# Expert weights in 1 MB chunks: a ring of 18 single slots in place of nine double ones

## The chip, the core and the metric

The kernel runs on one core of one Trainium2 chip. The metric is device time in microseconds of one execution, from three runs: median 1295.08 us, 1293.2 to 1295.19. Profiles are taken in a separate execution. Everything is in float32. In this text 1 MB is 1,048,576 bytes (the profile's own "MB" are 1,000,000 bytes).

## The reference

One layer over 256 latent tokens and 256 context tokens of width 1024. A mixer (a bidirectional gated linear recurrence beside a pooling branch) comes first; then a mixture of 32 experts, of which each token takes four. Every expert gets some tokens, so all of their weights are read: `w1` is 1024 x 2048, `w2` 1024 x 1024, 12 MB per expert, 384 MB in all.

```python
def moe(h, w_r, b_r, w1, b1, w2, b2):
    logits = (h @ w_r + b_r).astype(jnp.float32)
    top_v, top_i = lax.top_k(logits, TOP_K)
    top_w = jax.nn.softmax(top_v, axis=-1)
    comb = jnp.einsum('nk,nke->ne', top_w, jax.nn.one_hot(top_i, N_EXPERTS, dtype=jnp.float32)).astype(h.dtype)
    out = jnp.zeros_like(h)
    for e in range(N_EXPERTS):
        z = h @ w1[e] + b1[e]
        glu = jnp.minimum(z[:, :D_FF], SWIGLU_LIMIT)
        lin = jnp.clip(z[:, D_FF:], -SWIGLU_LIMIT, SWIGLU_LIMIT)
        act = glu * jax.nn.sigmoid(SWIGLU_ALPHA * glu) * (lin + 1)
        out = out + comb[:, e:e + 1] * (act @ w2[e] + b2[e])
    return out
```

## The kernel before

The kernel is written engine by engine, with semaphores between them; nothing reorders it. Its first 360 us are the mixer and the router. Then TensorE (`pe`) goes through 33 items. An item is one expert with up to 64 of its tokens; one expert with more tokens than that is run twice, as items 15 and 16, on weights loaded once.

In an item TensorE multiplies the gathered tokens `xg` with `w1` (`first_map`, 32 matmuls; the profile counts each float32 matmul twice, so 64), scatters the item before into the output sums (`scatter`), gathers the next item's tokens (`gather`), turns the activations of this one (`item`, L934) and multiplies them with `w2` (`second_map`, 16 matmuls). The last item does its second map in two halves of the output columns (`second_map_halves`). DVE and ACT compute SwiGLU in between.

Weights come through `arena`, 18 slots of 1 MB (8 KB in each of 128 partitions). `PAIRS` names nine pairs of neighbouring slots, which become a ring; an expert is six chunks of 2 MB (`CPI = 6`), four of `w1` and two of `w2`. In a `w1` chunk each partition holds two neighbouring rows of `w1`, in a `w2` chunk four of `w2`, so that a partition reads 16 KB in one piece (`expert_src`). That fixes which channels stand in which partition, and the transposes of tokens and activations pick their columns with a step of 2 or 4 to match.

SyncE (`sp`) issues all the expert loads in order, on one queue. Load n goes into pair n mod 9, and its semaphore `expert_landed[n mod 9]` is what TensorE waits for before the chunk's first matmul. TensorE counts `w_used` up after a chunk's last matmul, and SyncE waits for that count before it issues the load that takes the chunk's place. While the mixer runs, the slots hold other things, so the first nine loads wait for those one after another (L427 to L453): the last of them for the end of the output projection and for the tokens' normalisation. From the third expert on SyncE needs the routing result first (`items_ready`, L457). GpSimd loads 16 chunks of `w_mod` during the mixer on its own queue (L520), 8 KB in each partition; `w_in` comes in rows of 1 KB (L426), `w_out` in rows of 4 KB (L437).

Of the kernel before, what the change touches and what calls it, by code (L numbers as in the profile page):

```python
# [12 lines left out]
ds = bass.ds  # L13

P = 128
D = 1024
KT = D // P
# [12 lines left out]
SLOTS = 64  # L30
MORE = 16
FILL = (3, 1, 2)
CPI = 6
FETCHED = 2
TWICE = 15
NP = E + 1
# [7 lines left out]
CW = KT * CHUNK  # L44
BANK = 512
HALF = 512
NSLOT = 18
ACC, TMP, WIN, UT, XC, M2, ROWS_AT = 0, 2, 6, 8, 10, 16, 17
RING_SLOTS = [12, 13, 14, 15]
RING = len(RING_SLOTS)  # L50
MOD_SLOTS = [ACC, ACC + 1, TMP, TMP + 1, M2, ROWS_AT, TMP + 2, TMP + 3]
OUT_SLOTS = [XC, XC + 1, ACC, ACC + 1]
PAIRS = [UT, WIN, TMP, TMP + 2, RING_SLOTS[2], RING_SLOTS[0], XC, ACC, M2]
WSLOTS = len(PAIRS)
RING_CHUNKS = 4 + 2 * HEADS + 4 + 12 + 1 + 8
GM_SLOTS = [ROWS_AT, M2, XC, XC + 1]
GM_AT = [0, 1, 0, 1, 0, 1, 0, 2, 3, 0, 2, 3, 0, 2, 3, 0]
# [34 lines left out]
def build(nc, I, out):  # L92
    ctx = ExitStack()
    with ctx:
# [9 lines left out]
        def slot(n, w=CW):  # L104
            return arena[:, n * CW:n * CW + w]
# [61 lines left out]
        o = WIN * CW  # L167
# [14 lines left out]
        brow = {g: arena[:, TMP * CW + n * D:TMP * CW + (n + 1) * D] for n, g in enumerate(("g1", "sh2", "sc2", "g2"))}  # L182
        nrow = {g: arena[:, TMP * CW + (n + 4) * D:TMP * CW + (n + 5) * D] for n, g in enumerate(("g1", "sc2", "g2"))}

        wpair = [arena[:, n * CW:(n + 2) * CW] for n in PAIRS]
        w1_at = [w.rearrange("p (r n) -> p r n", r=2) for w in wpair]
        w2_at = [w.rearrange("p (r n) -> p r n", r=4) for w in wpair]

        sh2rw = RB[:, 0:KT * E].rearrange("p (k e) -> p k e", k=KT)
        sh2sum = RB[:, KT * E:KT * E + E]  # L190
# [140 lines left out]
        def chunk_used(n):  # L331

            kind, m = next(key for key, c in chunk_no.items() if c == n)
            if kind == "lru":
                return gates_done, m + 1
            if kind == "xr" and m == 0:
                return rows_used, 1
            if kind == "xr" and m == 1:
                return job_done, number["xr", 3] + 1
            if kind in ("xr", "pw"):  # L340
                m += {"xr": 1, "pw": 3}[kind]
            return job_done, number[kind, m] + 1
# [17 lines left out]
        def slot_of(i, c):  # L360

            return load_no(i, c) % WSLOTS

        def landed_at(i, c):

            if isinstance(i, int):
                return 16 * (load_no(i, c) // WSLOTS + 1)
            return i * 16 + 16 * ((LAST + c) // WSLOTS + 1 - FIXED)

        def expert_src(e, c):  # L370

            if c < 4:
                return I["exp_w1"][0, ds(e, 1), c * 256:(c + 1) * 256, :].rearrange("a (p r) n -> p (a r) n", r=2)
            return I["exp_w2"][0, ds(e, 1), (c - 4) * 512:(c - 3) * 512, :].rearrange("a (p r) n -> p (a r) n", r=4)

        def load_vectors(eng, names):

# [17 lines left out]
        def _(sp):  # L395
            def load_expert(q, e, c):
                s = (q * CPI + c) % WSLOTS
                sp.dma_start((w1_at if c < 4 else w2_at)[s], expert_src(e, c)).then_inc(expert_landed[s], 16)

            def load_mod(g):  # L400

# [11 lines left out]
            for n, parts in enumerate(chunks):  # L413
                if n < 2:
                    load_mod(n)
                if n >= RING:
                    sp.wait_ge(*chunk_used(n - RING))
                at = RING_SLOTS[n % RING] * CW
                for src, o in parts:
                    w = int(np.prod(src.shape)) // P  # L420
                    dst = arena[:, at + o:at + o + w]
                    if len(src.shape) == 4:
                        dst = dst.rearrange("p (g k n) -> p g k n", g=src.shape[1], k=src.shape[2])
                    else:
                        dst = dst.rearrange("p (k n) -> p k n", k=src.shape[1])
                    sp.dma_start(dst, src).then_inc(ring_landed[n % RING], 16)  # L426
                if n == chunk_no["pp", 2]:  # L427
                    sp.wait_ge(job_done, number["mp", 3] + 1)
                    load_expert(0, 0, 0)
                if n == chunk_no["pp", 3]:  # L430
                    sp.wait_ge(job_done, number["pw", 3] + 1)
                    load_expert(0, 0, 1)
                if n == chunk_no["rp", 0]:
                    sp.wait_ge(job_done, number["rs", 5] + 1)
                    sp.wait_ge(g2_part, 1)
                    for c in range(4):
                        sp.dma_start(wo_w[c], I["w_out"][0, c * 256:(c + 1) * 256, :].rearrange(  # L437
                            "(k p) n -> p k n", p=P)).then_inc(wo_landed, 16)
            sp.wait_ge(rows_ready, 1)
            load_expert(0, 0, 2)  # L440
            load_expert(0, 0, 3)
            sp.wait_ge(*chunk_used(chunk_no["rp", 1]))
            sp.wait_ge(*chunk_used(chunk_no["rp", 2]))
            load_expert(0, 0, 4)
            sp.wait_ge(*chunk_used(chunk_no["rp", 3]))
            load_expert(0, 0, 5)
            sp.dma_start(x1, I["x"][0].rearrange("(t p) d -> p t d", p=P)).then_inc(xres_landed, 16)
            sp.wait_ge(wo_done, 2 * TT)
            load_expert(1, 1, 0)
            load_expert(1, 1, 1)  # L450
            sp.wait_ge(ssq3_ready, 2 * TT)
            sp.wait_ge(v_ready, TT)
            load_expert(1, 1, 2)  # L453
            sp.dma_start(b2s, I["exp_b2"][0]).then_inc(b2_landed, 16)
            for q in range(1, E - 1):
                if q == FETCHED:
# [93 lines left out]
        def _(pe):  # L550
# [244 lines left out]
            def first_turn(q):  # L795

                pe.wait_ge(xgt_ready, q + 1)
                if q:
                    bank_read(7)
                for j in range(2 * q, 2 * q + 2):  # L800
                    last = nc.tensor.transpose(psum[1 + 6 * q][:, j * P:(j + 1) * P], xgt[:, q * 256 + j % 2:q * 256 + 256:2], ident[:, :])
                last.then_inc(xT_done, 1)

            def gather(n):
# [9 lines left out]
            def turn_tokens(n):  # L814

                pe.wait_ge(xgt_ready, n + 2)
                b = psum[4]
                for j in range(4):
                    last = nc.tensor.transpose(b[:, j * P:(j + 1) * P], xgt[:, j // 2 * 256 + j % 2:j // 2 * 256 + 256:2], ident[:, :])  # L819
                last.then_inc(xT_done, 1)  # L820

            def first_map(i, first=False):

                for c in range(4):
                    if first and c == 1:
                        turn_weights()
                        pe.wait_ge(xg_ready, 2)
                    s = slot_of(i, c)
                    pe.wait_ge(expert_landed[s], landed_at(i, c))
                    for r in range(2):  # L830
                        k = 2 * c + r
                        for q in range(2):
                            for h in range(2):
                                o = q * D + h * HALF
                                last = mm(psum[4 + q][h * SLOTS:(h + 1) * SLOTS, :], xg[:, k // 4, k % 4, :],  # L835
                                          w1_at[s][:, r, o:o + HALF], start=False, stop=(k == KT - 1))
                    last.then_inc(w_used, 1)

            def second_map(i):

                for c in range(2):
                    s = slot_of(i, 4 + c)
                    pe.wait_ge(expert_landed[s], landed_at(i, 4 + c))
                    for r in range(4):
                        for h in range(2):
                            last = mm(psum[6][h * SLOTS:(h + 1) * SLOTS, :], actT[:, c, r, :],  # L846
                                      w2_at[s][:, r, h * HALF:(h + 1) * HALF], start=(c == 0 and r == 0), stop=(c == 1 and r == 3))
                    last.then_inc(w_used, 1)

            def second_map_halves(i):  # L850

                for q in range(2):
                    for c in range(2):
                        s = slot_of(i, 4 + c)
                        if q == 0:
                            pe.wait_ge(expert_landed[s], landed_at(i, 4 + c))
                        for r in range(4):
                            for h in range(2):
                                o = h * HALF + q * 256
                                last = mm(psum[6 + q][h * SLOTS:(h + 1) * SLOTS, 0:256], actT[:, c, r, :], w2_at[s][:, r, o:o + 256],  # L860
                                          start=(c == 0 and r == 0), stop=(c == 1 and r == 3))
                    last.then_inc(y_half, 1)

            def scatter_halves(n):
# [48 lines left out]
            def item(i, first=False, last=False):  # L913
# [17 lines left out]
                if first:  # L931
                    pe.wait_ge(items_ready, 1)
                for j in range(4):
                    turned = nc.tensor.transpose(psum[7][:, j * P:(j + 1) * P], actf[:, j:HALF:4], ident[:, :])  # L934
                turned.then_inc(actT_done, 1)
                if not last:
                    turn_tokens(i + 1)
# [262 lines left out]
        def _(dve):  # L1200
# [366 lines left out]
            def item(i, last=False):  # L1567
# [5 lines left out]
                if not last:  # L1573
# [9 lines left out]
                    else:  # L1583
                        dve.wait_ge(gather_done, i)
                    one_hot(e1, r1)
                dve.wait_ge(w_used, i * CPI + 4)
                v.tensor_scalar(glu, psum[4][:, :], LIMIT, None, ALU.min).then_inc(glu_ready, 1)  # L1587
                step(v.tensor_scalar(lin, psum[5][:, :], LIMIT, -LIMIT, ALU.min, ALU.max), 1)
                dve.wait_ge(glu_ready, i + 1)
# [81 lines left out]
```

## Time and profile before

| | |
|---|---|
| median of 3 runs | 1295.08 us |
| the profiled execution's own time | 1293.98 us |
| its span, first to last instruction | 1291.7 us |
| granted TensorE clock, mean | 0.997 |
| TensorE busy | 1254.9 us, 97% of the span |
| DVE / ACT / GpSimd busy | 352.0 / 216.8 / 30.6 us |
| moved by DMA | 476.03 MB (of 1,000,000 bytes) |
| SyncE's queue alone | 454.23 MB, 85.4% of 16 engines' span |
| chain that ended last | PE 77%, DMA 14%, ACT 4%, DVE 4% |

The chain is followed back from the last instruction; its DMA part is the loads of expert weights (13%), its largest TensorE part the first map (L835, 28%) and the second map (L846, 15%). A busy TensorE is one that has matmuls in flight; what it waits for stands behind a row in square brackets.

### The profile page before, as it was taken

What the parts mean: (1) busy time and instruction counts of PE and PEld (TensorE: products, weight loads), DVE (VectorE), ACT (ScalarE), POOL (GpSimd) and SP (SyncE); (2) the same over time, 40 slices, a digit from 0 to 9 for tenths busy, and PEclk for the clock granted to TensorE, in tenths of its full rate; (3) what the DMA queues carried; (4) which work ended last, traced back from release to release, by engine and by line L of the source; (5) the groups of instructions that cost most, each with busy time, mean ns of one, the idle gap of its engine ahead of it and who ended that gap; (6) DMA issues with size and microseconds to landing.
All of it is one profiled execution on the core that took longest, in us unless ns stands there. A gap on an engine that the chain in (4) does not pass through costs nothing.

```text
span 1291.7 us, 14009 instructions
## 1 busy us (share of the span) xinstructions
PE 1254.9 (97%) x5726; PEld 548.3 (42%) x5726; DVE 352.0 (27%) x636; ACT 216.8 (17%) x368; POOL 30.6 (2%) x79
## 2 busy tenths in 40 slices
PE   5999999999999999999999999999999999999996
PEld 3445688888443333333333333333333333333332
DVE  4567787322441111211111211111211111211113
ACT  3166631110220100111000110100111000101001
POOL 1000000100000000000000000000000000000000
PEclk9999999999999999999999999999999999999998
DMA  9832568997399999999999999999999999999994
GB/s 354 264 129 80 197 216 308 373 348 270 126 392 376 429 426 426 427 429 428 428 426 427 427 428 428 414 429 427 428 427 427 428 427 428 428 426 428 428 426 205
DMA packets 74287, 476.03 MB, mean 369 GB/s; under 512 B 7184, under 2 KB 39120, under 8 KB 47600
## 3 DMA queue, kind: packets, MB, share of 16 engines
q1 hardware_dynamic: 68208, 454.23, 85.4%
q0 software_dynamic: 3312, 20.45, 4.2%
q8 instruction: 45, 0.74, 0.2%
q10 hardware_dynamic: 2704, 0.47, 0.2%
q14 instruction: 18, 0.15, 0.0%
HBM read 474.07 MB, written 1.05 MB: 368 GB/s over the span
## 4 chain that ended last, share of the span: by engine, by line
PE 77%; DMA 14%; ACT 4%; DVE 4%; issue 1%; SPq 0%; DVEq 0%; ACTq 0%
PE bank L835 28%; PE bank L846 15%; DMA arena<-in_exp_w 13%; PE bank L712 11%; PE bank L810 4%; PE bank L883 4%; PE bank L603 2%; PE bank L633 2%; PE bank L580 2%; PE bank L819 1%; PE bank L934 1%; PE bank L650 1%; ACT arena L1041 1%; ACT arena L1035 1%; ACT arena L1043 1%
## 5 line engine op out<-in xcount | busy, mean ns | idle before, releaser
L835 PE MATMUL bank<-arena,temps 128*64 128x512 f32 x2112 | 463.6, 594 | 9.4 <-DMA arena<-in_exp_w 9.4
L835 PEld LDWEIGHTS bank<-arena,temps 128*64 128x64 f32 x2112 | 147.7, 137 | 321.7 <-issue 300.4
L846 PE MATMUL bank<-arena,temps 128*64 128x512 f32 x1024 | 226.8, 595 | 0.1
L1587 DVE TENSOR_SCALAR temps<-bank 128x512 f32<-128x512 f32 x33 | 22.8, 692 | 666.7 <-PE bank L835 666.7
L846 PEld LDWEIGHTS bank<-arena,temps 128*64 128x64 f32 x1024 | 70.5, 137 | 133.6 <-issue 128.1
L712 PE MATMUL bank<-arena 128*128 128x256 f32 x512 | 111.2, 379 | 0.0
L1148 ACT ACTIVATE temps<-temps 128x512 f32<-128x512 f32 x33 | 20.8, 630 | 507.5 <-DVE temps L1587 507.5
L712 PEld LDWEIGHTS bank<-arena 128*128 128x128 f32 x512 | 97.3, 190 | 14.9 <-issue 1.9
L883 PE MATMUL bank<-temps,hot 64*128 64x512 f32 x256 | 63.6, 615 | 0.0
L810 PE MATMUL bank<-vtokb,hot 128*64 128x512 f32 x256 | 62.0, 605 | 0.0
L650 PE MATMUL bank<-arena 128*128 128x512 f32 x128 | 56.3, 593 | 0.4 <-ACT arena L1036 0.4
L1164 ACT ACTIVATE temps<-bank 128x512 f32<-128x512 f32 x32 | 19.1, 597 | 204.1 <-PE bank L846 204.1
L883 PEld LDWEIGHTS bank<-temps,hot 64*128 64x128 f32 x256 | 22.0, 186 | 41.0 <-issue 41.0
L1594 DVE COPY temps<-bank 128x512 f32<-128x512 f32 x33 | 22.8, 692 | 53.5 <-PE bank L934 53.5
L532 POOL COPY bsel<-ident 128x256 f32 (+1 forms) x33 | 13.8, 418 | 979.7 <-PE bank L835 920.1
L650 PEld LDWEIGHTS bank<-arena 128*128 128x128 f32 x128 | 24.2, 190 | 30.0 <-issue 29.9
L1315 DVE SCALAR_TENSOR_TENSOR arena<-arena,sT 128x2048 f32<-128x2048 f32 x14 | 32.7, 2351 | 15.5 <-DMA arena<-in_w_mod 15.3
L603 PE MATMUL bank<-b1r,bsel 32*64 32x512 f32 x264 | 35.9, 613 | 0.0
L810 PEld LDWEIGHTS bank<-vtokb,hot 128*64 128x64 f32 x256 | 15.5, 136 | 42.5 <-issue 42.5
L1141 ACT ACTIVATE temps<-bank 128x512 f32<-128x512 f32 x32 | 19.1, 597 | 76.2 <-PE bank L810 76.2
L934 PEld LDWEIGHTS bank<-ident,temps 128*128 128x128 f32 x132 | 18.5, 209 | 27.8 <-DVE temps L1592 27.1
L633 PE MATMUL bank<-arena 128*128 128x512 f32 x64 | 28.1, 595 | 1.3 <-DVE arena L1271 1.3
(268 smaller groups left out, 858.2 us busy)
## 6 DMA issues: line engine op xcount, KB each, us to landing
arena<-in_exp_w SPq DMA_DIRECT2D x192, 2048.0 KB, 24.2
arena<-in_w_in SPq DMA_DIRECT2D x20, 1024.0 KB, 6.0
arena<-in_w_mod POOLq DMA_DIRECT2D x16, 1024.0 KB, 7.6
arena<-in_w_mod SPq DMA_DIRECT2D x16, 512.0 KB, 11.2
arena<-in_w_pool_proj SPq DMA_DIRECT2D x4, 1024.0 KB, 9.0
arena<-in_w_rnn_proj SPq DMA_DIRECT2D x4, 1024.0 KB, 7.4
arena<-in_w_out SPq DMA_DIRECT2D x4, 1024.0 KB, 11.1
arena<-in_lru_wa SPq DMA_DIRECT2D x8, 256.0 KB, 2.8
```

Source lines behind the costliest of these rows:

```text
L580: last = mm(psum[2 * t + h][:, :], mgT[:, k, t * P:(t + 1) * P], wo_w[k // 2][:, k % 2, h * HALF:(h + 1) * HALF], start=(k == 0), stop=(k ...
L603: mm(psum[4 + q // 2][h * SLOTS:(h + 1) * SLOTS, :], bselq[r, q, :], b1r[r, :], start=True, stop=False)
L633: return mm(bank_of("xr", j)[:, :], w[:, k % 4, j * P:(j + 1) * P], uT[:, k, :], start=(k == 0), stop=(k == KT - 1))
L650: last = mm(psum[2 * q + j][:, :], w[:, q, k, j * P:(j + 1) * P], xc[:, 2 * h + k, :], start=(k == 0), stop=(k == 1))
L712: last = mm(b[:, j * SEQ:(j + 1) * SEQ], w[:, k, j * P:(j + 1) * P], src[:, k, :], start=(k == 0), stop=(k == KT - 1))
L810: last = mm(b[h * SLOTS:(h + 1) * SLOTS, :], sel[:, t, :], vtok[:, t, h * HALF:(h + 1) * HALF], start=(t == 0), stop=(t == TT - 1))
L835: last = mm(psum[4 + q][h * SLOTS:(h + 1) * SLOTS, :], xg[:, k // 4, k % 4, :], w1_at[s][:, r, o:o + HALF], start=False, stop=(k == KT - 1))
L846: last = mm(psum[6][h * SLOTS:(h + 1) * SLOTS, :], actT[:, c, r, :], w2_at[s][:, r, h * HALF:(h + 1) * HALF], start=(c == 0 and r == 0), s ...
L883: last = mm(psum[2 * t + h][:, :], gt[r, t * P:(t + 1) * P], yS[r, :], start=False, stop=False, skip_group_check=True)
L934: turned = nc.tensor.transpose(psum[7][:, j * P:(j + 1) * P], actf[:, j:HALF:4], ident[:, :])
L1315: v.scalar_tensor_tensor(acc[h], w, s_k, acc[h], ALU.mult, ALU.add).then_inc(gm_done, 1)
L1587: v.tensor_scalar(glu, psum[4][:, :], LIMIT, None, ALU.min).then_inc(glu_ready, 1)
```

## The change

Each expert is loaded in twelve chunks of 1 MB, eight of `w1` and four of `w2`, into 18 single slots in the same order of places, each with a semaphore of its own. A `w1` chunk is now 128 rows with one row (8 KB) per partition, a `w2` chunk 256 rows with two (8 KB). Matmuls, their number and their order are the same; TensorE waits and counts up after half as many. The transposes pick their columns in the new channel order. In the prologue each load waits for the release of its own slot: in place of one load that waits for two chunks of `w_rnn_proj`, there is one load behind each.

```diff
-CPI = 6
+CPI = 12
-PAIRS = [UT, WIN, TMP, TMP + 2, RING_SLOTS[2], RING_SLOTS[0], XC, ACC, M2]
-WSLOTS = len(PAIRS)
+SINGLES = [UT, UT + 1, WIN, WIN + 1, TMP, TMP + 1, TMP + 2, TMP + 3, *RING_SLOTS[1:], RING_SLOTS[0],
+           XC, XC + 1, ACC, ACC + 1, M2, ROWS_AT]
+WSLOTS = len(SINGLES)
...
-        wpair = [arena[:, n * CW:(n + 2) * CW] for n in PAIRS]
-        w1_at = [w.rearrange("p (r n) -> p r n", r=2) for w in wpair]
-        w2_at = [w.rearrange("p (r n) -> p r n", r=4) for w in wpair]
+        w1_at = [slot(n) for n in SINGLES]
+        w2_at = [slot(n).rearrange("p (r n) -> p r n", r=2) for n in SINGLES]
...
-            if c < 4:
-                return I["exp_w1"][0, ds(e, 1), c * 256:(c + 1) * 256, :].rearrange("a (p r) n -> p (a r) n", r=2)
-            return I["exp_w2"][0, ds(e, 1), (c - 4) * 512:(c - 3) * 512, :].rearrange("a (p r) n -> p (a r) n", r=4)
+            if c < KT:
+                return I["exp_w1"][0, ds(e, 1), c * P:(c + 1) * P, :].rearrange("a p n -> p (a n)")
+            return I["exp_w2"][0, ds(e, 1), (c - KT) * 256:(c - KT + 1) * 256, :].rearrange("a (p r) n -> p (a r) n", r=2)
...
             sp.wait_ge(rows_ready, 1)
-            load_expert(0, 0, 2)
-            load_expert(0, 0, 3)
-            sp.wait_ge(*chunk_used(chunk_no["rp", 1]))
-            sp.wait_ge(*chunk_used(chunk_no["rp", 2]))
-            load_expert(0, 0, 4)
-            sp.wait_ge(*chunk_used(chunk_no["rp", 3]))
-            load_expert(0, 0, 5)
+            for c in range(4, KT):
+                load_expert(0, 0, c)
+            for c in range(4):
+                sp.wait_ge(*chunk_used(chunk_no["rp", c]))
+                load_expert(0, 0, KT + c)
             sp.dma_start(x1, I["x"][0].rearrange("(t p) d -> p t d", p=P)).then_inc(xres_landed, 16)
             sp.wait_ge(wo_done, 2 * TT)
-            load_expert(1, 1, 0)
-            load_expert(1, 1, 1)
+            for c in range(4):
+                load_expert(1, 1, c)
             sp.wait_ge(ssq3_ready, 2 * TT)
             sp.wait_ge(v_ready, TT)
-            load_expert(1, 1, 2)
+            load_expert(1, 1, 4)
+            load_expert(1, 1, 5)
...
-                for c in range(4):
-                    if first and c == 1:
+                for k in range(KT):
+                    if first and k == 2:
                         turn_weights()
                         pe.wait_ge(xg_ready, 2)
-                    s = slot_of(i, c)
-                    pe.wait_ge(expert_landed[s], landed_at(i, c))
+                    s = slot_of(i, k)
+                    pe.wait_ge(expert_landed[s], landed_at(i, k))
+                    for q in range(2):
+                        for h in range(2):
+                            o = q * D + h * HALF
+                            last = mm(psum[4 + q][h * SLOTS:(h + 1) * SLOTS, :], xg[:, k // 4, k % 4, :],
+                                      w1_at[s][:, o:o + HALF], start=False, stop=(k == KT - 1))
+                    last.then_inc(w_used, 1)
...
-                    turned = nc.tensor.transpose(psum[7][:, j * P:(j + 1) * P], actf[:, j:HALF:4], ident[:, :])
+                    turned = nc.tensor.transpose(psum[7][:, j * P:(j + 1) * P], actf[:, j // 2 * 256 + j % 2:j // 2 * 256 + 256:2], ident[:, :])
```

`second_map` and `second_map_halves` change in the same way (four chunks of two row groups in place of two of four), and the token transposes now read neighbouring columns.

SyncE's order, from the last loads of the first filling of the ring to the first that take a used slot's place, before:

```order
L398 DMA arena<-in_exp_w 128x4096 [waits wo_done]
L398 DMA arena<-in_exp_w 128x4096
L398 DMA arena<-in_exp_w 128x4096 [waits v_ready,ssq3_ready]
L454 DMA b2buf<-in_exp_b 32x1024
L398 DMA arena<-in_exp_w 128x4096 [waits w_used] x3
L458 TENSOR_LOAD tabE [waits items_ready]
```

and now:

```order
L398 DMA arena<-in_exp_w 128x2048 [waits wo_done]
L398 DMA arena<-in_exp_w 128x2048 x3
L398 DMA arena<-in_exp_w 128x2048 [waits v_ready,ssq3_ready]
L398 DMA arena<-in_exp_w 128x2048
L455 DMA b2buf<-in_exp_b 32x1024
L398 DMA arena<-in_exp_w 128x2048 [waits w_used] x6
L459 TENSOR_LOAD tabE [waits items_ready]
```

Each load became two of half the width; the waits for the mixer's results stand at the same bytes, and each of the six loads behind `b2buf` waits for a count of its own.

TensorE's order at the end of one item's second map and the start of the next first map, before:

```order
L846 MATMUL bank<-arena,temps 64x512 [waits expert_landed5]
L846 MATMUL bank<-arena,temps 64x512 x7
L603 MATMUL bank<-b1r,bsel 64x512 [waits gt_ready,xg_ready,bsel_ready]
L603 MATMUL bank<-b1r,bsel 64x512 x3
L835 MATMUL bank<-arena,temps 64x512 [waits expert_landed6]
L835 MATMUL bank<-arena,temps 64x512 x7
```

and now:

```order
L845 MATMUL bank<-arena,temps 64x512 [waits expert_landed10]
L845 MATMUL bank<-arena,temps 64x512 x3
L845 MATMUL bank<-arena,temps 64x512 [waits expert_landed11]
L845 MATMUL bank<-arena,temps 64x512 x3
L604 MATMUL bank<-b1r,bsel 64x512 [waits gt_ready,xg_ready,bsel_ready]
L604 MATMUL bank<-b1r,bsel 64x512 x3
L834 MATMUL bank<-arena,temps 64x512 [waits expert_landed12]
L834 MATMUL bank<-arena,temps 64x512 x3
L834 MATMUL bank<-arena,temps 64x512 [waits expert_landed13]
L834 MATMUL bank<-arena,temps 64x512 x3
```

The matmuls stand as before; a wait for a landed chunk stands ahead of every four and not every eight of them.

## Rows read from the trace of the kernel before

**Rows 1.** The page: 40 slices of 32.3 us, DMA busy in tenths and GB/s.

```profile
DMA  9832568997399999999999999999999999999994
GB/s 354 264 129 80 197 216 308 373 348 270 126 392 376 429 426 426 427 429 428 428 426 427 427 428 428 414 429 427 428 427 427 428 427 428 428 426 428 428 426 205
```

**Rows 2.** Timeline of TensorE, 690 to 845 us: start, duration, instructions, wait before.

```profile
695.43 13.95 PE L835 MATMUL bank<-arena,temps 128*64 128x512 f32 x64
...
722.79 10.52 PE L835 MATMUL bank<-arena,temps 128*64 128x512 f32 x48
...
750.74 7.09 PE L835 MATMUL bank<-arena,temps 128*64 128x512 f32 x32
758.14 3.65 PE L835 MATMUL bank<-arena,temps 128*64 128x512 f32 x16 [0.32 <-DMA arena<-in_exp_w]
763.04 3.65 PE L835 MATMUL bank<-arena,temps 128*64 128x512 f32 x16 [1.24 <-DMA arena<-in_exp_w]
...
780.11 7.09 PE L835 MATMUL bank<-arena,temps 128*64 128x512 f32 x32
```

**Rows 3.** Waits of TensorE, 690 to 830 us, then 830 to 1270: total, times, longest.

```profile
PE bank L835 <- DMA arena<-in_exp_w: 3.5, 5, 1.2
...
PE bank L835 <- DMA arena<-in_exp_w: 5.9, 7, 1.3
```

**Rows 4.** Windows: busy us and count of each engine, clock, DMA share, GB/s.

```profile
43.00:45.00 2.00, 2.00 (x6) 0.83 (x5) 1.01 (x4) 1.71 (x4) 0.00 (x0) 1.00 1.00 418
...
156.00:158.00 2.00, 2.00 (x6) 0.95 (x5) 0.26 (x1) 1.98 (x3) 0.53 (x1) 1.00 1.09 384
...
159.00:160.50 1.50, 1.50 (x5) 0.71 (x4) 1.00 (x1) 0.95 (x2) 0.00 (x0) 1.00 1.03 431
...
276.00:284.00 8.00, 8.00 (x39) 7.03 (x37) 0.70 (x2) 0.00 (x0) 0.00 (x0) 1.00 1.05 390
...
366.00:368.50 2.50, 2.50 (x14) 0.74 (x12) 1.49 (x7) 0.00 (x0) 0.40 (x1) 1.00 0.56 111
388.00:391.50 3.50, 3.50 (x18) 1.15 (x16) 0.00 (x0) 0.00 (x0) 0.00 (x0) 1.00 0.37 80
...
420.00:620.00 200.00, 199.88 (x954) 68.19 (x952) 30.70 (x63) 19.47 (x36) 3.22 (x8) 1.00 1.01 428
...
810.00:820.00 10.00, 10.00 (x50) 3.39 (x48) 0.00 (x0) 0.00 (x0) 0.40 (x1) 1.00 0.94 387
...
1270.00:1274.50 4.50, 2.85 (x20) 1.50 (x19) 2.33 (x4) 1.88 (x3) 0.00 (x0) 1.00 0.53 222
```

**Rows 5.** The page: DMA issues, KB each, median us from issue to landing.

```profile
arena<-in_exp_w SPq DMA_DIRECT2D x192, 2048.0 KB, 24.2
arena<-in_w_in SPq DMA_DIRECT2D x20, 1024.0 KB, 6.0
```

**Rows 6.** SyncE's timeline; the last row is the landing of the 366.60 load alone.

```profile
270.64 2.85 SPq L437 DMA_DIRECT2D arena<-in_w_out  x4
...
348.86 7.01 SPq L398 DMA_DIRECT2D arena<-in_exp_w  x3
355.92 0.43 SPq L454 DMA_DIRECT2D b2buf<-in_exp_b  x1
...
366.60 27.39 SPq L398 DMA_DIRECT2D arena<-in_exp_w  x6
...
DMA to landing us min/median/max: 8.0/8.0/8.0
```

**Rows 7.** Timeline of TensorE, item 0: first chunk and second map.

```profile
362.92 3.65 PE L835 MATMUL bank<-arena,temps 128*64 128x512 f32 x16
...
386.40 7.09 PE L846 MATMUL bank<-arena,temps 128*64 128x512 f32 x32
```

**Rows 8.** Timeline of TensorE, last item: fourth chunk, transposes, second map.

```profile
1265.26 3.65 PE L835 MATMUL bank<-arena,temps 128*64 128x512 f32 x16 [1.25 <-DMA arena<-in_exp_w]
...
1271.92 0.75 PE L934 MATMUL bank<-ident,temps 128*128 128x128 f32 x4 [1.08 <-DVE temps L1592]
...
1273.45 7.13 PE L860 MATMUL bank<-arena,temps 128*64 128x256 f32 x64 [0.56 <-DVE temps L1594]
```

More of the change, by code:

```diff
@@ L397, in load_expert @@
                 s = (q * CPI + c) % WSLOTS
-                sp.dma_start((w1_at if c < 4 else w2_at)[s], expert_src(e, c)).then_inc(expert_landed[s], 16)
+                sp.dma_start((w1_at if c < KT else w2_at)[s], expert_src(e, c)).then_inc(expert_landed[s], 16)
             def load_mod(g):
@@ L429, in _ @@
                     load_expert(0, 0, 0)
+                    load_expert(0, 0, 1)
                 if n == chunk_no["pp", 3]:
                     sp.wait_ge(job_done, number["pw", 3] + 1)
-                    load_expert(0, 0, 1)
+                    load_expert(0, 0, 2)
+                    load_expert(0, 0, 3)
                 if n == chunk_no["rp", 0]:
@@ L800, in first_turn @@
                 for j in range(2 * q, 2 * q + 2):
-                    last = nc.tensor.transpose(psum[1 + 6 * q][:, j * P:(j + 1) * P], xgt[:, q * 256 + j % 2:q * 256 + 256:2], ident[:, :])
+                    last = nc.tensor.transpose(psum[1 + 6 * q][:, j * P:(j + 1) * P], xgt[:, j * P:(j + 1) * P], ident[:, :])
                 last.then_inc(xT_done, 1)
@@ L818, in turn_tokens @@
                 for j in range(4):
-                    last = nc.tensor.transpose(b[:, j * P:(j + 1) * P], xgt[:, j // 2 * 256 + j % 2:j // 2 * 256 + 256:2], ident[:, :])
+                    last = nc.tensor.transpose(b[:, j * P:(j + 1) * P], xgt[:, j * P:(j + 1) * P], ident[:, :])
                 last.then_inc(xT_done, 1)
             def first_map(i, first=False):
-                for c in range(4):
-                    if first and c == 1:
+                for k in range(KT):
+                    if first and k == 2:
@@ L826, in first_map @@
                         turn_weights()
                         pe.wait_ge(xg_ready, 2)
-                    s = slot_of(i, c)
-                    pe.wait_ge(expert_landed[s], landed_at(i, c))
[L830 to L836, printed above, removed]
+                    s = slot_of(i, k)
@@ L837, in first_map @@
+                    pe.wait_ge(expert_landed[s], landed_at(i, k))
[4 more added lines that the diff above has]
+                                      w1_at[s][:, o:o + HALF], start=False, stop=(k == KT - 1))
                     last.then_inc(w_used, 1)
             def second_map(i):
[L841 to L844, printed above, removed]
+                for c in range(4):
+                    s = slot_of(i, KT + c)
+                    pe.wait_ge(expert_landed[s], landed_at(i, KT + c))
+                    for r in range(2):
@@ L845, in second_map @@
                         for h in range(2):
-                            last = mm(psum[6][h * SLOTS:(h + 1) * SLOTS, :], actT[:, c, r, :],
-                                      w2_at[s][:, r, h * HALF:(h + 1) * HALF], start=(c == 0 and r == 0), stop=(c == 1 and r == 3))
+                            last = mm(psum[6][h * SLOTS:(h + 1) * SLOTS, :], actT[:, c // 2, c % 2 * 2 + r, :],
+                                      w2_at[s][:, r, h * HALF:(h + 1) * HALF], start=(c == 0 and r == 0), stop=(c == 3 and r == 1))
@@ L852, in second_map_halves @@
                 for q in range(2):
-                    for c in range(2):
-                        s = slot_of(i, 4 + c)
+                    for c in range(4):
+                        s = slot_of(i, KT + c)
                         if q == 0:
-                            pe.wait_ge(expert_landed[s], landed_at(i, 4 + c))
-                        for r in range(4):
+                            pe.wait_ge(expert_landed[s], landed_at(i, KT + c))
+                        for r in range(2):
                             for h in range(2):
                                 o = h * HALF + q * 256
-                                last = mm(psum[6 + q][h * SLOTS:(h + 1) * SLOTS, 0:256], actT[:, c, r, :], w2_at[s][:, r, o:o + 256],
-                                          start=(c == 0 and r == 0), stop=(c == 1 and r == 3))
+                                last = mm(psum[6 + q][h * SLOTS:(h + 1) * SLOTS, 0:256], actT[:, c // 2, c % 2 * 2 + r, :],
+                                          w2_at[s][:, r, o:o + 256], start=(c == 0 and r == 0), stop=(c == 3 and r == 1))
                     last.then_inc(y_half, 1)
@@ L1585, in item @@
                     one_hot(e1, r1)
-                dve.wait_ge(w_used, i * CPI + 4)
+                dve.wait_ge(w_used, i * CPI + KT)
                 v.tensor_scalar(glu, psum[4][:, :], LIMIT, None, ALU.min).then_inc(glu_ready, 1)
```

## The prediction, made before the run

> **What bounds the kernel now.** I read the page's 40 slices first [rows 1]. From the fourteenth slice on, at about 420 us, the DMA engines are at 9 tenths with 426 to 429 GB/s in nearly every slice, while before it there are holes. TensorE is busy too, so the second view is TensorE's own timeline, to see which of the two waits. Early on an item starts every 27.36 us (695.43 to 722.79) without a wait; from then on the third and fourth chunk of each first map wait for their load, 0.3 and 1.2 us, and an item takes 29.37 us (750.74 to 780.11) [rows 2]. That is the transfer time: one expert is 12 MB of 1,048,576 bytes, and at 428 GB/s 1 MB takes 2.450 us, twelve take 29.4. The table of waits says the same: 3.5 us between 690 and 830 us and 5.9 us after [rows 3]; before 690 it lists no such wait. So TensorE eats up a lead until about item 12, and then the stream of weights sets the pace up to the last item. The waits look small (9.4 us together), yet the end is set by when the last byte comes; anything that changes the rate or the start of the stream reaches the end one to one. The queue's depth belongs to this: an expert load lands 24.2 us after its issue though it moves for 4.9 us [rows 5], so some five loads stand in line.
>
> **What the change doesn't touch.** The same bytes, matmuls and ring size. TensorE gets 12 waits per item in place of 6; between two chunks that have both landed the matmuls run on without a gap, 32 of them in 7.09 us [rows 2], which is two chunks. SyncE issues 384 loads in place of 192. Its issues are 4.9 us apart on average and become 2.45 us apart; four w_out loads went out back to back in 2.85 us [rows 6], so I charge nothing; if that cover went, the queue of five loads would stand in between. The transposes read their operand with another stride: 0.75 us for four [rows 8], the same count; at most tenths of a microsecond at the end, zero taken.
>
> **Term 1, the rate.** Before, each partition of a load takes 16 KB in one piece; after it is 8 KB. So 1 MB becomes 128 pieces over 16 engines, 8 per engine, where it was 4, and one completion per MB and engine in place of a half. The trace has no stream of 8 KB pieces on SyncE's queue, so I bound it by the windows [rows 4], all of them at a DMA share of 1.0 or more:
> - 16 KB pieces (420 to 620): 428 GB/s, 2.450 us per MB.
> - 1 KB pieces of w_in (156 to 158): 384 GB/s, 2.731 us. That is 60 more pieces per engine for 0.281 us, 4.7 ns each. With 4 more pieces and half a completion, taken as half a piece: +0.021 us per MB.
> - 4 KB pieces of w_out (276 to 284): 390 GB/s, 2.689 us: 12 more pieces for 0.239 us, 20 ns each; 4 more would be +0.080 us per MB.
> - 8 KB pieces of w_mod from GpSimd's queue: 418 GB/s (43 to 45) and 431 (159 to 160.5), 2.509 and 2.433 us: +0.059 and -0.017, in the middle +0.021. These windows are of 2 us and hold few pieces, so they are rough.
> The ends are 0 and +0.080. I take +0.028, a little over the two middles of 0.021, because the upper end lies so much further off than the lower. It applies to the stream from the second hole on: 384 MB less the 18 of the first fill and the 8 of the next burst, 358 MB. 358 x 0.028 = +10.0 us (0 to +28.6).
>
> The Trainium skill bears on this. "DMA: Bandwidth & Descriptors" (Why small descriptors are slow) states that each packet carries a fixed overhead inside a trn2 DMA engine, which speaks for the 4.7 to 20 ns per piece above. The same page (iDMA fabric) gives 408.7 GB/s for one core's stream from SyncE in loads of 1 MiB with 4 KiB rows. By that, 4 KB pieces cost +0.116 us per MB, a third of it is +0.039, and the sum's first term would be an estimated +13.8 us. No run here shows that figure; w_out's row is below it.
>
> **Term 2, the start of the stream.** The first fill is all 18 MB in both; its last loads go out at 348.86 to 355.9. Then the engines run dry, since the next load waits for the first chunk of item 0: it goes out at 366.60 [rows 6], when the 16 matmuls of the first chunk (362.92, 3.65 us) are done [rows 7]. In the 2.5 us from 366 only 111 GB/s move [rows 4]. With single slots the first release comes after 8 matmuls, 1.82 us earlier. The second hole is at 388 to 391.5 (80 GB/s): by then everything that item 0's first map freed has come, and the next slot is freed by the first chunk of its second map, which starts at 386.40 and takes 3.5 us [rows 7]. Again the first half chunk frees 1 MB 1.8 us earlier. It is the same 1.8 us, not a second one, since the stream behind the second hole starts that much earlier either way. Afterwards slots are freed faster than they fill (12 MB per 27.36 us against 29.4), so it is kept: -1.8 us.
>
> **Term 3, the item without release.** Item 15 runs one expert for the first time and frees nothing. At 810 to 820 the stream falls to 387 GB/s [rows 4]: 10 x (1 - 387/428) = 0.96 us lost, before item 16's first chunk has freed a slot. With half chunks item 15 ends its first map 1.8 us sooner after its last load, and the first release comes 1.8 us sooner. That covers it: -1.0 us.
>
> **Term 4, the end.** In the last item the fourth chunk of w1 lands at 1265.26, and 16 matmuls of 3.65 us follow before SwiGLU, transposes and the second map, which starts at 1273.45 [rows 8]. After, only the last 1 MB is still to be worked when the last w1 byte lands: 8 matmuls, -1.8 us. What is late next: the last byte of w2. The windows end the stream at 1274 or so (222 GB/s over 1270 to 1274.5 [rows 4]), 8.7 us behind that w1 landing. The second map would start 8.19 - 1.82 = 6.4 us behind it and needs its last 1 MB three quarters into its first half (7.13 us in all [rows 8], so 2.7 us later), at 9.1. It just fits, so the whole 1.8 us counts.
>
> **Sum.** 1293.98 us of the profiled execution (span 1291.70, 2.28 around it) + 10.0 - 1.8 - 1.0 - 1.8 = 1299.4 us. The median of the three runs is 1295.08, 1.1 above the profiled one, so against it the change costs 4.3 us, +0.33%. What a measurement of this kernel tells from no change is about 0.2%, 2.6 us: "same" is 1292.5 to 1297.7.
>
> **Rivals.**
> - *The piece's size costs nothing.* For it: the window of 431 GB/s, and 428 GB/s may be a ceiling of bytes. Against: both other piece sizes on the same queue are slower than 428. Then the three gains stand alone: 1293.98 - 4.6 = 1289.4, faster. The point from which it decides is 4.6/358 = 0.013 us per MB, at 423 to 426 GB/s.
> - *It about cancels*, 0.006 to 0.020 us per MB: 1291.5 to 1296.5. For it: 4.7 ns per piece is an average over 60 small pieces, and 0.020 is my own middle.
> - *8 KB pieces behave like w_out's.* +28.6 - 4.6: 1318. For it: the longest clean window of another size, 8 us. Against: w_out's loads also start a new place in HBM every 4 KB, which these don't, and the 1 KB pieces beat them.
> - *A fixed time per load shows.* A lone load lands 8.0 us after its issue [rows 6] where 4.9 are transfer, 3.1 us over. "DMA: Bandwidth & Descriptors" (Measured) has 341 GB/s for one load of 1 MB and 425 for one of 16 MB. If a mere tenth of the 3.1 us showed for the 192 added loads, that would be +60 us, 1349. Against: w_in's loads are of 1 MB and run at 384 GB/s with 1 KB pieces; a queue of five to ten loads hides it.
>
> **Chances and range.** Forecast (0.020 to 0.050 us per MB, 1296.5 to 1307.3): 0.55. About cancels: 0.17. Costs nothing or under 0.006: 0.15. Like w_out's or above 0.050: 0.11. Fixed time: 0.02. Faster by over 0.2%: all of "costs nothing" and a little of "cancels", 0.18. Same: most of "cancels" and the low edge of the forecast, 0.20. Slower: the rest, 0.62. The range of 8 in 10 takes the forecast and the case that cancels whole, and ends a little inside both outer cases: 1290 to 1309.
>
> **What would show it.** GB/s in the slices from 420 us on: 423 for the forecast, 428 if size is free, 415 like w_out. Items in the starved part 29.7 us apart and not 29.37; the first waits on a load before item 12, since the lead is eaten faster. The first reload at 364.8 and not 366.6, no dip near 815 us, and 8 rather than 16 matmuls behind the last w1 landing. I am wrong if the rate stays at 428, or if SyncE's queue shows waits other than those on used slots.

## The result, and the profile after

The changed kernel takes 1306.47 us, median of 4 runs (1304.93 to 1308.22), against 1295.13 (1293.2 to 1297.03): ratio 1.0087, 95% interval 1.0073 to 1.0101. It is slower, by 11.3 us where 4.3 were forecast; the time lies in the range of 1290 to 1309. A second series of the same kernel gave 1.0088 (1.0072 to 1.0104). The profiled execution took 1305.76 us, 11.8 over that of before; its span of 1303.9 us is 12.2 longer.

The slices of the changed kernel's page (32.6 us each), to be laid beside [rows 1]:

```profile
DMA  9832568997299999999999999999999999999994
GB/s 351 262 128 88 187 230 308 373 337 316 98 366 421 421 421 421 421 421 420 421 421 421 421 421 421 421 421 421 420 421 421 421 421 421 420 421 421 421 421 193
```

The stream settles at 421 where it was 428, one slice earlier, and the slice of 414 is gone. Windows of the changed kernel, columns as in [rows 4]; the windows from 800 to 840 hold the stretch of the old dip:

```profile
420.00:620.00 200.00, 199.84 (x956) 67.69 (x954) 30.69 (x63) 19.46 (x36) 3.21 (x8) 1.00 1.01 421
...
800.00:820.00 20.00, 19.98 (x100) 6.85 (x98) 3.70 (x9) 2.69 (x5) 0.40 (x1) 1.00 1.01 421
820.00:840.00 20.00, 19.98 (x100) 6.87 (x98) 4.38 (x9) 2.69 (x5) 0.00 (x0) 1.00 1.01 420
366.00:368.50 2.50, 2.50 (x14) 0.77 (x12) 1.92 (x11) 0.00 (x0) 0.00 (x0) 1.00 0.98 302
388.00:391.50 3.50, 3.50 (x18) 1.15 (x16) 0.24 (x2) 0.00 (x0) 0.00 (x0) 1.00 0.41 117
```

TensorE's timeline, two items in the starved part and, below the dots, the last item. It answers to [rows 2, 8]:

```profile
752.98 9.02 PE L834 MATMUL bank<-arena,temps 128*64 128x512 f32 x40
762.54 1.94 PE L834 MATMUL bank<-arena,temps 128*64 128x512 f32 x8 [0.55 <-DMA arena<-in_exp_w]
...
782.77 9.03 PE L834 MATMUL bank<-arena,temps 128*64 128x512 f32 x40
...
1277.40 1.94 PE L834 MATMUL bank<-arena,temps 128*64 128x512 f32 x8 [0.55 <-DMA arena<-in_exp_w]
...
1283.87 2.81 PE L859 MATMUL bank<-arena,temps 128*64 128x256 f32 x24 [0.56 <-DVE temps L1593]
1288.30 4.54 PE L859 MATMUL bank<-arena,temps 128*64 128x256 f32 x40 [1.62 <-DMA arena<-in_exp_w]
1292.77 2.12 PE L871 MATMUL bank<-temps,hot 64*128 64x256 f32 x16
```

An item takes 29.79 us (782.77 - 752.98); 12 chunks of 1,048,576 bytes at 421 GB/s take 29.9. The last row is the final scatter; before, it was this one, 12.26 us earlier:

```profile
1280.51 2.12 PE L872 MATMUL bank<-temps,hot 64*128 64x256 f32 x16
```

TensorE's waits from 690 to 830 us and from 830 to 1290: 5.7 and 10.8 us where [rows 3] has 3.5 and 5.9, and a new one in the last second map. (The second stretch ends later than that of [rows 3], because the last item does.)

```profile
PE bank L834 <- DMA arena<-in_exp_w: 5.7, 11, 0.6
...
PE bank L834 <- DMA arena<-in_exp_w: 10.8, 20, 0.6
PE bank L859 <- DMA arena<-in_exp_w: 1.6, 1, 1.6
```

**The 12.26 us in pieces.** The two rates are rounded, and over 350 MB the rounding alone is worth a microsecond, so I added up the trace's packets of expert weights one by one. The point at which 350 MB are still to come is reached at 410.88 for 412.23, 1.35 us earlier: the earlier first reload, although item 0 itself starts 0.5 later (363.40 for 362.92). From there to the last 4 MB the stream takes 863.23 us for 850.89, +12.34. Of that about +13.2 are the lower rate (0.038 us per MB) and -0.8 the filled dip. The last `w1` load then lands 3.25 us behind that point, where it was 2.10: +1.15. Together +12.14, which is what the rows of the last `w1` load show (1277.40 for 1265.26). Then the way to the second map is 6.47 us and not 8.19, -1.72, and the second map takes 8.90 to the scatter and not 7.06, +1.84, most of it the new wait of 1.62.

### The profile page after: what moved, and what is told of

Same layout as the page of the kernel before. It is cut to its first block, busy times and chain, and to the rows that moved or that the text cites. A ratio compares the mean times of both kernels' runs of the same rounds, so it can differ in the third digit from the quotient of the medians.

```text
span 1303.9 us, 14566 instructions
## 1 busy us (share of the span) xinstructions
PE 1257.6 (96%) x5726; PEld 542.6 (42%) x5726; DVE 351.8 (27%) x636; ACT 216.8 (17%) x368; POOL 30.5 (2%) x79
## 4 chain that ended last, share of the span: by engine, by line
PE 59%; SPq 23%; DMA 9%; ACT 4%; DVE 3%; issue 2%; DVEq 0%; ACTq 0%
SPq L398 22%; PE bank L834 19%; PE bank L713 11%; PE bank L845 10%; DMA arena<-in_exp_w 8%; PE bank L811 3%; PE bank L882 3%; PE bank L634 2%; PE bank L581 2%; PE bank L604 1%; PE bank L651 1%; PE bank L933 1%; PE bank L820 1%; ACT arena L1040 1%; ACT arena L1034 1%
## 5 line engine op out<-in xcount | busy, mean ns | idle before, releaser
L834 PE MATMUL bank<-arena,temps 128*64 128x512 f32 x2112 | 469.1, 596 | 16.5 <-DMA arena<-in_exp_w 16.4
L1586 DVE TENSOR_SCALAR temps<-bank 128x512 f32<-128x512 f32 x33 | 22.8, 691 | 679.5 <-PE bank L834 679.5
L1593 DVE COPY temps<-bank 128x512 f32<-128x512 f32 x33 | 22.8, 691 | 53.4 <-PE bank L933 53.4
L651 PEld LDWEIGHTS bank<-arena 128*128 128x128 f32 x128 | 24.3, 190 | 30.0 <-issue 29.9
```

The costliest lines, as they stand in the source:

```text
L651: last = mm(psum[2 * q + j][:, :], w[:, q, k, j * P:(j + 1) * P], xc[:, 2 * h + k, :], start=(k == 0), stop=(k == 1))
```

## The experiments

All ratios are to the kernel before on the same chip. One reading of noise first: in some executions the granted clock falls to its lower level (0.5, 1.2 GHz) for some microseconds between 380 and 392 us, during item 0. The profiled executions of experiments 2, 4 and 12 have it, so their comparison rests on medians. In experiment 2's, item 1 starts at 396.15; in its repetition 11, which has the full clock and the same start of item 0, at 393.10. The times follow it: for the kernel before, executions with a mean clock of 0.998 took 1294.1 us on average, those with 0.995 took 1297.0. "At equal mean clock" below stands for one slope fitted through all executions, 0.9 us for 0.001 of mean clock. This row is experiment 4's:

```profile
388.00:391.50 3.50, 3.50 (x10) 0.96 (x11) 0.95 (x4) 0.37 (x2) 0.00 (x0) 0.55 0.24 98
```

**1. The streams by themselves.** Seven streams of 40 MB from SyncE, with nothing beside them.

```diff
+    ("pieces of 16 KB, loads of 2 MB", w1_rows, 2, True, 20, 9),
+    ("pieces of 8 KB, loads of 2 MB", w1_rows, 2, False, 20, 9),
+    ("pieces of 8 KB, loads of 1 MB", w1_rows, 1, True, 40, 18),
+    ("pieces of 4 KB, loads of 1 MB", w2_rows, 2, False, 40, 18),
+    ("pieces of 32 KB, loads of 4 MB", w1_rows, 4, True, 10, 4),
+    ("pieces of 16 KB, loads of 2 MB, four slots", w1_rows, 2, True, 20, 4),
+    ("pieces of 8 KB, loads of 1 MB, six slots", w1_rows, 1, True, 40, 6),
```

> Leaves out the whole layer: seven streams of expert weights on SyncE's queue, nothing else, so only its rates count. Theory (each piece costs a fixed time of its engine): from 428 GB/s at 16 KB and 421 at 8 KB a piece costs about 10 ns, so 2 MB loads in 8 KB pieces run at 421 like 1 MB loads in 8 KB pieces, 4 KB pieces at about 408, 32 KB pieces at about 431. Rival (each load costs a fixed time): 2 MB loads in 8 KB pieces run at 428, 1 MB loads at 421 whatever the piece, 4 MB loads at 431. Rival (the queue's depth holds the stream back): the streams with four and with six slots are slower than the same pieces with nine and eighteen; the theory has them equal.

Windows of its one execution, one in the middle of each stream (columns: start and end, us, GpSimd, clock, DMA share, GB/s):

```profile
20.00:100.00 80.00, 0.00 (x0) 1.00 1.01 428
120.00:200.00 80.00, 0.00 (x0) 1.00 1.01 422
220.00:300.00 80.00, 0.00 (x0) 1.00 1.01 422
320.00:400.00 80.00, 0.00 (x0) 1.00 1.03 410
432.00:512.00 80.00, 0.00 (x0) 1.00 0.99 422
530.00:610.00 80.00, 0.00 (x0) 1.00 1.01 429
630.00:710.00 80.00, 0.00 (x0) 1.00 1.01 422
```

Loads of 2 MB and of 1 MB in 8 KB pieces are equal, so a load costs nothing of its own that shows; four slots are as fast as nine and six as eighteen, so the depth doesn't either. From 16 to 8 KB 4 more pieces per engine and MB cost 0.035 us (8.7 ns each), from 8 to 4 KB 8 more cost 0.073 (9.1 ns). The fifth row, of 32 KB pieces, reads 422 because that stream ends inside the window, at 510 us; over 430 to 505 it reads 431, and a window counts whole pieces of 1.2 us and is coarse. With four slots, though, a load waits for its three forerunners, so its time to landing is four transfers. That gives 38.8/4 = 9.7 us per 4 MB, 2.425 per MB; the same reading of the four slots of 16 KB gives 19.6/8 = 2.45, as its window does.

```profile
DMA to landing us min/median/max: 7.6/38.8/38.8
...
DMA to landing us min/median/max: 19.6/19.6/19.6
```

**2 and 11. Loads of 2 MB in 8 KB pieces.** Ring, releases and waits of before, channel order of after. The transposes change with it, as in the changed kernel.

```diff
-                return I["exp_w1"][0, ds(e, 1), c * 256:(c + 1) * 256, :].rearrange("a (p r) n -> p (a r) n", r=2)
-            return I["exp_w2"][0, ds(e, 1), (c - 4) * 512:(c - 3) * 512, :].rearrange("a (p r) n -> p (a r) n", r=4)
+                return I["exp_w1"][0, ds(e, 1), c * 256:(c + 1) * 256, :].rearrange("a (r p) n -> p (a r) n", r=2)
+            return I["exp_w2"][0, ds(e, 1), (c - 4) * 512:(c - 3) * 512, :].rearrange("a (s p r) n -> p (a s) (r n)", s=2, r=2)
...
```

> The kernel before (2 MB loads, nine pairs) with the new channel order, so that a partition reads its 16 KB as two pieces of 8 KB. Theory (cost per piece): the stream runs at 421 GB/s and none of the gains of single slots are there: 1294 + 358 x 0.038 = 1308 us, a little above the changed kernel. Rival (cost per load): 428 GB/s and 1294 us as before.

> 2 MB loads in 8 KB pieces, nine pairs, once more, in more rounds. What single slots are worth at this rate is the difference to the changed kernel beside it. Theory (start 1.8, dip up to 1.0, end given back): 2 to 3 us, so 1308.5 to 1309.5. Rival (all three gains of the forecast, 4.6): 1311. Rival (none): 1306.5.

1308.93 us, 1.0097 (1.0081 to 1.0114), and again 1308.79, 1.0107 (1.0088 to 1.0126). The stream:

```profile
420.00:620.00 200.00, 199.83 (x958) 67.73 (x956) 30.70 (x63) 19.46 (x36) 3.04 (x8) 1.00 1.01 421
```

The size of the pieces alone makes the whole loss and more. The single slots themselves are a gain of some 2.5 us by the medians (1306.47 and 1306.29 against these two). That figure is good to about 1 us: the four series spread by 2 to 5 us each, and compared at equal mean clock they lie 2.1 apart.

**3. `w2` in 4 KB pieces**, on the changed kernel; the transposes of the activations change with it.

```diff
-            return I["exp_w2"][0, ds(e, 1), (c - KT) * 256:(c - KT + 1) * 256, :].rearrange("a (p r) n -> p (a r) n", r=2)
+            return I["exp_w2"][0, ds(e, 1), (c - KT) * 256:(c - KT + 1) * 256, :].rearrange("a (r p) n -> p (a r) n", r=2)
...
```

> The changed kernel with w2 in 4 KB pieces (two rows 128 apart per partition) in place of 8 KB; loads of 1 MB as they were. Theory (about 10 ns per piece): a third of the stream goes from 2.491 to 2.57 us per MB, 8 more pieces each, so 119 MB x 0.08 = +9.5 us on the changed kernel, about 1316. Rival (4 KB pieces cost what w_out's window showed, 390 GB/s): 119 x 0.20 = +24 us, 1330. Rival (cost per load): no change, 1306. Beside it: if SyncE's queue holds a fixed number of pieces, fewer loads stand in line and the median from issue to landing falls from 26.0 us to about 20; if it holds a fixed number of loads it stays.

1317.25 us, 1.0155 (1.0134 to 1.0176): 10.8 over the changed kernel, where 9.5 and 24 were the two answers. The rate is 417, and a load lands 20.7 us after its issue, not 26.0:

```profile
420.00:620.00 200.00, 199.23 (x958) 66.83 (x956) 30.69 (x63) 19.46 (x36) 3.22 (x8) 1.00 1.02 417
...
DMA to landing us min/median/max: 4.7/20.7/28.9
```

**4. Release in pairs**, on the changed kernel.

```diff
-                    last.then_inc(w_used, 1)
+                    if k % 2:
+                        last.then_inc(w_used, 2)
...
-                    last.then_inc(w_used, 1)
+                    if c % 2:
+                        last.then_inc(w_used, 2)
```

> The changed kernel, but TensorE counts w_used up by two after every second chunk, so slots are released in pairs as before; landing stays at 1 MB. Theory (term 2 and half of term 3 were real gains): the first reload goes out 1.8 us later, the dip of 0.5 to 1 us near 815 may come back, and the end is 2 to 3 us later, 1308.5 to 1309.5. Rival (the earlier release buys nothing, since the stream's end is set elsewhere): 1306.5.

1309.15 us, 1.0098 (1.0081 to 1.0116): 2.7 more than the changed kernel and the same as experiment 2. The first reload goes out at 366.68; in the changed kernel it went out at 365.37. So the earlier release is all that the single slots were worth (1.8 us at equal mean clock), and of the finer landing no gain shows: the two series with landings of 1 MB and of 2 MB lie 0.2 us apart, with a spread of 2 to 3 us in each.

**5 to 9 and 12. The gains without the loss.** 16 KB pieces and pairs as before, but TensorE counts up after each half of a chunk and chosen loads are split into two halves of 1 MB (8 KB pieces), each with its own release and landing.

```diff
+SPLIT = [(1, 3), (1, 4), (2, 1), (2, 2), (2, 3), (2, 4), (16, 3), (16, 4)]
+TAIL = [3, 5]
...
+                            for h in range(2):
+                                sp.wait_ge(w_used, used + 1 + h)
+                                load_half(q, e, c, h, extra)
...
```

`SPLIT` names loads by expert and chunk (both counted from 0), `TAIL` chunks of the last two experts. That makes twelve split loads in 5 and 12 (their expectations say fourteen), the first six of `SPLIT` in 6, the four of the tail in 7, fourteen loads and no tail in 8, and in 9 the same with chunk 3 of the last two experts.

> The kernel before (16 KB pieces, 2 MB loads, nine pairs), but fourteen loads are split into two halves of 1 MB with a release and a landing of their own: the six that refill the ring first, the two behind the item that frees nothing, and the fourth and sixth chunk of the last two experts; TensorE counts up after every half. Theory (the gains of single slots are real and only the piece's size costs): stream at 428 GB/s, start -1.8 us, dip near 815 us -1.0, end -1.3 (the last w2 load bounds it), together -4 us: 1291 us. Rival (the gains aren't there when the rate stays): 1295.

> Only the six first refills are split. Theory: first reload at about 364.8 us in place of 366.6, everything behind it 1.8 us earlier, 1293.3 us. Rival: the second hole takes it back, 1295.

> Only the fourth and sixth chunk of the last two experts are split. Theory: 8 matmuls and not 16 behind the last w1 landing, and the second map then waits at most some tenths for w2: -1.3 to -1.8 us, 1293.6. Rival (as in the changed kernel's trace, the last w2 load comes later than the engines' mean and takes the gain back): 1295.

> The mixed kernel without its split tail; split are the six refills behind item 0 and eight behind the item that frees nothing, so that both holes and the dip are covered. Theory (holes are worth what the stream gains in them, 1.3 us at the start in the trace of the mixed kernel and 0.5 to 1 at 815 us): 1293.2 against 1295.2, stream ahead of the kernel before by about 2 us from 250 MB on. Rival (nothing kept): 1295.2.

> The same, and the fourth chunk of the last two experts split; the last w2 loads stay at 2 MB. Theory (the split tail failed because the last load of 1 MB drains late: 4.6 to 5.8 us for the last MB of every kernel that ends in a 1 MB load, 4.1 to 4.9 where it is one of 2 MB): another 0.5 to 1.3 us off, 1292.3. Rival (the end hangs on the last w2 byte, whatever the w1 chunks do): 1293.2 like the kernel beside it.

> The mixed kernel once more (fourteen split loads). If its 0.9989 was real: 1293 and a ratio of 0.998 to 0.9995. If it was the luck of one series, since its two relatives without the split w2 load came out at 1.0002: 1295 and a ratio about 1.

| split | median us | ratio (95% interval) |
|---|---|---|
| 5: start, dip, tail | 1293.13 | 0.9989 (0.998 to 0.9998) |
| 12: the same again | 1294.01 | 0.9993 (0.9984 to 1.0002) |
| 6: start | 1295.06 | 0.9997 (0.9987 to 1.0006) |
| 7: tail | 1295.62 | 0.9997 (0.9988 to 1.0006) |
| 8: start, longer dip | 1295.56 | 1.0002 (0.9994 to 1.0011) |
| 9: the same and `w1` of the tail | 1296.1 | 1.0002 (0.9992 to 1.0013) |

The rate stays (428, 427 and 427 GB/s over 420 to 620 in 5, 6 and 7), but the gains that the expectations of 5 to 9 put at 1.3 to 4 us don't come. The first reload is early in experiment 6, yet the last `w1` chunk comes no more than 0.3 us sooner than in [rows 8]:

```profile
364.91 5.96 SPq L415 DMA_DIRECT2D arena<-in_exp_w  x4
```

```profile
1265.00 3.65 PE L867 MATMUL bank<-arena,temps 128*64 128x512 f32 x16 [1.24 <-DMA arena<-in_exp_w]
```

Its stream is 1.1 us ahead with 350 MB to come (411.15 for 412.23) and 0.8 ahead with 4 MB to come (1262.30 for 1263.12). It loses the first 0.3 behind item 15, where it runs a bit drier, 380 GB/s over 810 to 820 where it was 387; the next 0.6 go at the end, since the last `w1` load lands 2.7 us behind the 4 MB point and not 2.1. Whether that is chance in one execution these runs don't tell.

```profile
810.00:820.00 10.00, 10.00 (x48) 3.30 (x46) 0.00 (x0) 0.00 (x0) 0.40 (x1) 1.00 0.93 380
```

The tail in experiment 7 and in 9, each the last second map:

```profile
1278.20 4.54 PE L897 MATMUL bank<-arena,temps 128*64 128x256 f32 x40 [1.22 <-DMA arena<-in_exp_w]
```

```profile
1278.65 7.09 PE L897 MATMUL bank<-arena,temps 128*64 128x256 f32 x48 [2.72 <-DMA arena<-in_exp_w]
```

Where the second map starts earlier, it waits for the last `w2` load, 1.2 to 2.7 us, in a 2 MB load (9) as in 1 MB ones (5 and 7); in 12 its first 24 matmuls take 4.50 us and not 3.13, and 0.2 of wait is left. In 8 it starts no earlier and still waits 1.1, since that load lands 11.3 us behind the last `w1` load, where it was 9.8 before. Of the six series only one lies clear of 1, its repetition doesn't, and the variant with more of the holes covered is not faster. The 22 executions of 5 and 12 lie 0.8 us below the kernel before at equal mean clock, so a small part of the gain seems real; one of more than about 0.1% was not found.

**10. The changed kernel again**, the yardstick of 11: 1306.29 us.

> The changed kernel once more, as the yardstick of the kernel with 2 MB loads in 8 KB pieces beside it: 1306 to 1307, ratio 1.0087 as before.

## Why the prediction was right, and where its sizes were off

**What bounds the kernel: right.** A slower stream moved the end by its whole amount, and TensorE's longer waits (16.5 us on the first map in place of 9.4) are how that reaches TensorE and not a cost beside it. The first of them came in item 12 (707.37) where it was in item 13 (733.67). One thing was put too simply: TensorE isn't starved up to the last item. Item 16 needs no new weights, and behind it the items start 27.4 us apart again until item 28 (in the changed kernel 27.3, until item 25); only the stream runs on throughout, but for the dip.

**Term 1: right in kind, over a quarter too small.** It was put at 0.028 us per MB and measures 0.038 to 0.039 in the kernel (427.6 and 420.9 GB/s before rounding) and 0.035 in the stream by itself. That makes some 13.8 us of 358 MB and not 10.0. The mistake is in the middle value of 0.021. It came from the 1 KB pieces, whose 60 more cost 4.7 ns each, and that price doesn't carry over: between 16 and 4 KB a piece costs 9 ns. The second support, two windows of 2 us on GpSimd's queue (418 and 431), was too rough: they lie on both sides of the 422 measured here. The w_out row, at the other end, was dearer than the clean stream of 4 KB pieces (390 GB/s against 410); what slows `w_out` wasn't tried. The Trainium skill's rate in "DMA: Bandwidth & Descriptors" (iDMA fabric), 408.7 GB/s with 4 KiB rows, agrees with the 410 measured here, and the +0.039 us per MB estimated from it was nearer than my own value.

**Terms 2 and 3: right.** The first reload went out 1.7 us earlier against item 0 (365.37 - 363.40 = 1.97 behind its start, 3.68 before), the first hole carries 302 GB/s in place of 111, and the dip is gone. Experiments 2, 4, 10 and 11 value both together at 2.5 to 2.9 us by their medians and at about 2 at equal mean clock, against 2.8 forecast. The mixed kernels, though, show less: the same early reloads bring 0.1 us in the medians of experiment 6.

**Term 4: wrong.** "It just fits, so the whole 1.8 us counts" is the step that failed. The last `w2` load was put 8.7 us behind the last `w1` landing, from a window that shows when the sixteen engines' mean rate ends, and by the same paragraph it is needed at 9.1. The trace of before has its landing: issued at 1252.2 and landed 22.8 us later, at 1275.0, 9.8 us behind.

```profile
L398 SPq DMA_DIRECT2D arena<-in_exp_w x1: 332/332/332, 1252.2 to 1252.2; - x1
...
DMA to landing us min/median/max: 22.8/22.8/22.8
```

In the changed kernel it came 10.9 us behind (1288.30 - 1277.40). The engines don't finish together. Their share falls over 6 us (columns as in [rows 4]), the counts of the last load's semaphore come in from 1286.2 to 1288.3, and TensorE goes on with the last of them:

```profile
1280.00:1282.00 2.00, 1.26 (x6) 0.19 (x2) 1.77 (x4) 0.63 (x1) 0.00 (x0) 1.00 0.72 299
...
1284.00:1286.00 2.00, 2.00 (x20) 1.35 (x21) 0.00 (x0) 1.23 (x2) 0.00 (x0) 1.00 0.53 225
1286.00:1288.30 2.30, 0.68 (x8) 0.15 (x5) 0.00 (x0) 0.00 (x0) 0.00 (x0) 1.00 0.05 14
```

The term is +0.1 us and not -1.8, and experiment 4, with the same finer landing and no finer release, stands where experiment 2 stands.

**The sum with measured sizes:** 13.2 for the rate, -1.35 for the start (with the later item 0 of that execution in it), -0.8 for the dip, +1.15 for the later landing of the last `w1` load, which the forecast didn't have, and +0.1 for the end: 12.3 us against 12.26 in the trace. The forecast's own total also has a slip. Its terms add up to +5.4 us; the 4.3 came from setting a time built on the profiled execution (1293.98) against the median (1295.08). Like with like, +5.4 was forecast and +11.8 measured between the profiled executions, +11.3 between the medians. The range held because it was wide; its middle was less than half of what came.

**The rivals.** "Costs nothing" and "about cancels" fall with 421 GB/s; "like w_out's" falls with 421 and 410; "a fixed time per load" falls with the equal rates of 1 MB and 2 MB loads. The chance of 0.62 for slower was on the right side. Not foreseen at all was that SyncE's queue gets full (below). The prediction had named it as a sign of being wrong ("if SyncE's queue shows waits other than those on used slots"), and it appeared. It cost nothing that shows, since the engines had work throughout (a share of 1.01), but "I charge nothing" for SyncE's issues was right for another reason than the one given.

**Open.** Why the last landings lag the mean by 1 to 3 us more in some executions than in others; why the earlier release is worth about 2 us beside 8 KB pieces and so little in the mixed kernels; and how much of the mixed kernel's 1 to 2 us is real.

## What to carry to other kernels

When the profile shows the DMA engines at a share of 1 over hundreds of microseconds, ask of a change first what it does to the bytes that a partition reads in one piece, and only then to the number of loads; here 1.6% of the rate cost 13 us, and finer slots gave back about 2. Price such a change by the nearest sizes of piece, measured on a long stretch; a price per piece from far smaller ones came out at half. A gain in front of the last wait has to be checked against the last landing of the slowest engine, not against the end of the mean rate.

## What the runs showed of the hardware

- A piece costs its engine 9 ns beyond its bytes between 4 and 16 KB (410, 422, 428 GB/s), 4.7 ns on average from 16 KB down to 1 KB (384), and 32 KB pieces are a hundredth faster still (2.425 against 2.450 us per MB).
- SyncE's queue takes a limited amount of work, and the limit goes more by pieces than by loads. Before, an issue never took over 0.6 us; in the changed kernel the median is 1.5 us and the longest 4.9, in experiment 2 the longest 8.0. In the stream of 8 KB pieces and 1 MB loads 27.4 us from issue to landing are 11 loads of 8 pieces per engine, 88; with 2 MB loads 33.1 us are 6.7 loads of 16, 107; with 4 KB pieces 18.6 us are 7.3 loads of 16, 116. So neither count is constant, but that of pieces comes nearer. The changed kernel's chain of waits books this as 23% "SPq", though the rate didn't suffer from it. Issues of the two kernels, before and after, each with its times from issue to landing:

```profile
L398 SPq DMA_DIRECT2D arena<-in_exp_w x192: 328/333/580, 251.6 to 1252.2; - x192
...
DMA to landing us min/median/max: 7.5/24.2/40.2
```

```profile
L398 SPq DMA_DIRECT2D arena<-in_exp_w x384: 327/1534/4932, 252.2 to 1262.1; - x192
...
DMA to landing us min/median/max: 4.7/26.0/28.5
```
